# The last splits of two out-projections by token tile, and five products that nothing reads

## The chip, the cores and the metric

One core of a Trainium2 chip runs the whole program. TensorE multiplies and transposes, VectorE and ScalarE compute, GpSimd prepares small tables, and the queue of SyncE starts nearly all transfers from the chip's memory. In the rows they are PE, DVE, ACT, POOL and SP. The metric is the device time of one execution in microseconds (us).

## The reference

Two transformer blocks over 256 tokens of width 1024, all in float32. What matters here of the first block is the way from the heads to the experts:

```python
mixed = jnp.concatenate([rmsnorm(o_m, g_out_mla[i]), rmsnorm(o_s, g_out_sb[i])], axis=-1)
h = h + mixed @ w_o[i]
h = h + moe(rmsnorm(h, g_moe[i]), w_router[i], b_router[i], w_gu[i], b_gu[i], w_dn[i], b_dn[i])
```

`moe` takes 32 router logits of each token, keeps the top four, and applies those experts (1024 to 2048, a clamped SwiGLU, 1024 to 1024), weighted by a softmax of the four logits. Of the second block:

```python
mix = jnp.concatenate([attn, lru], axis=-1) @ w_out[l].astype(h.dtype)
x = x + rms_norm(mix, g_post_mix[l])
h = rms_norm(x, g_pre_ffn[l])
up = causal_dwconv(h @ w_up[l].astype(h.dtype), w_conv_ffn[l], b_conv_ffn[l])
```

## The kernel before

Tokens lie in two tiles of 128 (t = 0, 1), the width in two halves of 512 columns (n = 0, 1), so an out-projection has four results of 128 x 512, one PSUM bank each: `U_o[t][n]` in the first block, `U_mix[t][n]` in the second. The engines run their own instruction lists, each strictly in the order in which it is written, and wait for one another through semaphores.

**Split weights.** A dense product in float32 is made of three fast ones (`mm3`): the weights are a rounded high part and a low part, and so is the other operand. Each load of weights is a "split", numbered 0 to 66 in the order of use. `split(s)` on ACT (L766) writes its high part into one of two halves of the tile W (half s modulo 2), and DVE then writes its low part (L1224). Before `split(s)` writes, it waits for `pair_free[s - 2]`: the last product that reads split s - 2, since both use the same half of W.

**An out-projection** has four splits of two 128-deep slices of the contraction each: 12 to 15 in the first block, 30 to 33 in the second. A split has 24 products (2 slices, 2 token tiles, 2 halves, 3 of `mm3`). `rows_in` runs the first three of them slice by slice over all four results, and the last one result by result (`by_tile`), so that the four results are complete six products apart.

**After the first out-projection** DVE adds each result to `h` (`add_o`, L1491), PE transposes `h` (L2228), ACT and DVE copy the transposes out of PSUM, and PE forms the logits (L2236, 32 columns each). For every token tile DVE finds the top four and writes a mask `mk` (L1526 to L1538, with the semaphore `s_mk`). PE sums the masks into positions (L2245, L2246, L2248), DVE turns them into the selection (L1542, L1564), and with it PE gathers the experts' tokens (L2260) from `uhi` and `ulo`, the high and low parts of the rows that ACT (`rows_hi`, L926) and DVE (`rows_lo`, L1506) write into half 0 and 1 of W. The gathers are followed by `up(x)` (L2293) and `down(x)` (L2333) for each expert x. SP loads the experts' weights into a ring; a place is loaded again when the products that read it have been counted in `s_used`, two slices of 128 to a place.

**After the second out-projection** ACT squares each result with its sum (`square_rows`, L1139) and takes roots (L784, L789), DVE multiplies by the gain (`gained`, L1842), takes the reciprocal and adds to `h` (`add_rows`, L1851). ACT then squares `h` of a token tile (`square_h`, L1147), and its rows are scaled (token tile 0 by ACT, L1156, tile 1 by DVE, L1870), transposed by PE (L2537), and written as high parts by ACT (L1167, 16 times) and low parts by DVE (L1881). From there to the end PE runs the feed-forward part (L2008, L1937). On ACT the call `split(34)`, the first weights of the feed-forward part, stands directly in front of `square_rows` of token tile 0.

## Time and profile before

| | |
|---|---|
| median of 3 runs | 1412.57 us (1411.61 to 1415.88) |
| the profiled execution | 1414.68 us |
| its span | 1412.9 us |
| PE busy | 1285.8 us (91%) |
| DVE busy | 489.1 us (35%) |
| ACT busy | 400.7 us (28%) |
| read from memory | 478.39 MB, 340 GB/s over the span |

The profiled execution is 2.1 us above the median of the runs. Its span leaves out 1.8 us around it. The busy shares are means over stages of different kinds: dense stages with TensorE at work all the time at both ends, and between 360 and about 1070 us a stretch in which the experts' weights flow at 426 to 429 GB/s. The granted clock is a share of 2.4 GHz: 1.00 is 2.4 GHz, 0.50 is 1.2 GHz. PEld is TensorE's loading of the fixed operand.

### The profile page before, as it was taken

Reading aid. Unit: us, or ns where it says so; the run is one execution under the profiler, and the core shown is the slowest. Engines: PE = TensorE matmul, PEld = TensorE weight load, DVE = VectorE, ACT = ScalarE, POOL = GpSimd, SP = SyncE. Lnnn points to the kernel's source line nnn. Section 1 sums busy time; section 2 is a strip of 40 time slices with the busy share of each in tenths; the row PEclk is TensorE's granted clock in tenths of the full one; section 3 lists DMA queues with packets and bytes.
Section 4 is the critical chain, followed back from the end, with each engine's and each line's share of the span. In section 5 each row is a group of like instructions: output and inputs, shape, how many; then the busy total and the mean of one; then the engine's idle time right before and its main releaser. Section 6 shows DMA issues by size and latency. Waiting matters only on the chain.

```text
span 1412.9 us, 16571 instructions
## 1 busy us (share of the span) xinstructions
PE 1285.8 (91%) x6969; PEld 738.8 (52%) x6969; DVE 489.1 (35%) x735; ACT 400.7 (28%) x641; POOL 59.0 (4%) x115
## 2 busy tenths in 40 slices
PE   7989999999999889988888888888888999899998
PEld 7878543333333333333333333333324898799986
DVE  5795412111211112111121111211113777777765
ACT  5674312100111001110010100101003756755554
POOL 4001000000000000000000000000000510000000
PEclk9998899999999999999999999999999999999999
DMA  9437699999999999999999999999999964355520
GB/s 341 166 125 293 228 383 428 430 425 429 427 426 429 427 429 427 427 428 428 426 428 428 427 428 428 427 427 429 427 427 374 264 222 142 126 182 184 189 103 30
DMA packets 78474, 480.79 MB, mean 340 GB/s; under 512 B 5504, under 2 KB 40475, under 8 KB 53568
## 3 DMA queue, kind: packets, MB, share of 16 engines
q1 hardware_dynamic: 75904, 474.76, 82.9%
q0 software_dynamic: 2496, 4.96, 1.6%
q8 instruction: 57, 0.93, 0.3%
q14 instruction: 17, 0.14, 0.0%
HBM read 478.39 MB, written 1.31 MB: 340 GB/s over the span
## 4 chain that ended last, share of the span: by engine, by line
PE 51%; DMA 40%; DVE 4%; ACT 3%; issue 1%; DVEq 0%; SPq 0%; ACTq 0%
DMA arena<-in_w_dn_dram 38%; PE ps L1937 23%; PE ps L2333 11%; PE ps L2293 10%; DMA ring<-in_w_dn_dram 2%; PE ps L2260 1%; PE ps L2349 1%; DVE W L1224 1%; PE ps L1945 1%; PE ps L2450 1%; ACT arena L898 0%; PE ps L2217 0%; ACT arena L947 0%; PE ps L2304 0%; ACT W L766 0%
## 5 line engine op out<-in xcount | busy, mean ns | idle before, releaser
L2293 PE MATMUL ps<-ring,arena 128*64 128x512 f32 x1392 | 315.3, 597 | 11.8 <-DMA ring<-in_w_gu_dram 11.8
L2293 PEld LDWEIGHTS ps<-ring,arena 128*64 128x64 f32 x1392 | 98.7, 137 | 207.9 <-issue 175.4
L1937 PE MATMUL ps<-X,W 128*128 128x256 f32 x1560 | 189.1, 283 | 2.0 <-DVE W L1230 1.7
L1937 PEld LDWEIGHTS ps<-X,W 128*128 128x128 f32 x1560 | 187.8, 192 | 3.1 <-DVE W L1230 2.2
L1573 DVE TENSOR_SCALAR arena<-ps 128x512 f32<-128x512 f32 x32 | 22.1, 692 | 478.3 <-PE ps L2293 478.3
L1937 PE MATMUL ps<-W,X 128*128 128x512 f32 (+2 forms) x780 | 172.7, 381 | 3.8 <-DVE W L1224 1.9
L1224 DVE TENSOR_TENSOR W<-ring,W 128x2048 fp32r<-128x2048 f32 (+2 forms) x64 | 144.9, 2265 | 75.3 <-ACT W L766 75.3
L2333 PE MATMUL ps<-ring,arena 128*64 128x512 f32 x648 | 145.9, 595 | 22.9 <-DMA ring<-in_w_dn_dram 22.9
L1937 PEld LDWEIGHTS ps<-W,X 128*128 128x128 f32 x780 | 142.1, 188 | 31.8 <-DVE W L1224 4.0
L2293 PE MATMUL ps<-arena 128*64 128x512 f32 x656 | 150.5, 601 | 0.0
L960 ACT ACTIVATE arena<-arena 128x512 f32<-128x512 f32 x32 | 20.2, 631 | 459.3 <-DVE arena L1573 459.3
L766 ACT ACTIVATE W<-ring 128x2048 fp32r<-128x2048 f32 (+2 forms) x65 | 122.7, 1888 | 84.1 <-PE ps L1937 83.1
L2333 PEld LDWEIGHTS ps<-ring,arena 128*64 128x64 f32 x648 | 48.4, 137 | 117.6 <-issue 115.8
L2333 PE MATMUL ps<-arena 128*64 128x512 f32 x376 | 85.8, 598 | 24.7 <-DMA arena<-in_w_dn_dram 24.7
L1601 DVE SCALAR_TENSOR_TENSOR X<-ps,arena,X 128x512 fp32r<-128x512 f32 x32 | 24.0, 751 | 221.7 <-ACT X L973 221.7
L973 ACT ACTIVATE X<-ps,arena 128x512 fp32r<-128x512 f32 x32 | 22.0, 689 | 260.4 <-PE ps L2333 260.4
L2293 PEld LDWEIGHTS ps<-arena 128*64 128x64 f32 x656 | 47.5, 138 | 90.9 <-issue 88.7
L2333 PEld LDWEIGHTS ps<-arena 128*64 128x64 f32 x376 | 25.1, 136 | 84.9 <-DMA arena<-in_w_dn_dram 43.2
L2260 PEld LDWEIGHTS ps<-X,W 128*128 128x128 f32 x256 | 33.9, 198 | 25.5 <-issue 24.9
L714 POOL CAST W<-arena 128x128 fp32r<-128x128 f32 x32 | 9.4, 296 | 870.0 <-PE ps L2293 852.1
L2349 PE MATMUL ps<-X,W 64*128 64x512 f32 x256 | 39.3, 425 | 6.5 <-DVE X L1601 6.5
L2304 PE MATMUL ps<-ident,arena 128*128 128x128 f32 x128 | 21.4, 291 | 25.6 <-ACT arena L947 25.6
(348 smaller groups left out, 996.6 us busy)
## 6 DMA issues: line engine op xcount, KB each, us to landing
ring<-in_w_gu_dram SPq DMA_DIRECT2D x87, 2048.0 KB, 22.4
ring<-in_w_dn_dram SPq DMA_DIRECT2D x40, 2048.0 KB, 24.9
arena<-in_w_gu_dram SPq DMA_DIRECT2D x39, 2048.0 KB, 20.6
arena<-in_w_dn_dram SPq DMA_DIRECT2D x23, 2048.0 KB, 25.6
ring<-in_w_up_dram SPq DMA_DIRECT2D x22, 1024.0 KB, 5.1
ring<-in_w_in_dram SPq DMA_DIRECT2D x15, 1024.0 KB, 12.9
ring<-in_w_down_dram SPq DMA_DIRECT2D x11, 1024.0 KB, 4.9
ring<-in_w_o_dram SPq DMA_DIRECT2D x4, 1024.0 KB, 5.0
```

The lines of the kernel that those rows point to most:

```text
L766: e.activation(halved(s)[0], loads[n][0], ACT.Copy).then_inc(s_hi, 1)
L960: e.activation(sig, glu, ACT.Sigmoid, scale=1.702).then_inc(s_sig, 1)
L973: e.activation(yhi[x % 2], ps[:, DB, :], ACT.Copy, scale=gs[:, x:x + 1]).then_inc(s_yhi, 1)
L1224: e.tensor_tensor(lo, loads[SPL[s]][0], hi.bitcast(F32), ALU.subtract).then_inc(s_lo, 1)
L1573: e.tensor_scalar(glu, whole(gb), 7.0, None, ALU.min).then_inc(s_glu, 1)
L1601: e.scalar_tensor_tensor(out=ylo[x % 2], in0=ps[:, DB, :], scalar=gs[:, x:x + 1], in1=yhi[x % 2].bitcast(F32), op0=ALU.mult, op1=ALU.subtr ...
L1937: y = e.matmul(o, l, r, start=start and i == 0, stop=stop and i == 2)
L2260: y = e.matmul(ps[:, x[0], a * 256:(a + 1) * 256], part[:, t, k * P:(k + 1) * P], Sr[j % 2][:, t], start=part is uhi and t == 0, stop=part ...
L2293: y = e.matmul(ps[c * 64:c * 64 + 64, use[0], :], xs[:, k, c0:c0 + CAP], w[:, half * D + c * 512:half * D + (c + 1) * 512], start=False, s ...
L2304: y = e.transpose(ps[:, TB, j * P:(j + 1) * P], actv[:, j * P:(j + 1) * P], ident[:, :])
L2333: y = e.matmul(ps[c * 64:c * 64 + 64, DB, :], a, w[:, c * 512:(c + 1) * 512], start=kk == 0, stop=kk == KD - 1)
L2349: y = e.matmul(ps[:, b, :], GTr[x // 2 % 2][q, x % 2, t * P:(t + 1) * P], part[x % 2][q, :], start=x == 0 and part is yhi, stop=x == NE - ...
```

## The change

Three things are changed.

1. **First out-projection.** Splits 14 and 15 are run by token tile: on three results (0,0), (0,1), (1,0) split 14 and then split 15, then the eight transposes of token tile 0, and only then splits 14 and 15 on (1,1). The other transposes stand around the first half of the logits. DVE and ACT take their steps in a matching order, and `rows_hi` waits until split 14 has been read for the last time.
2. **Five products that nothing reads** (`kept_busy`): 128x128 by 128x512, from `uhi`, into a bank that a later gather overwrites. Two stand between the mask products of token tile 0 and that of tile 1, three behind the latter.
3. **Second out-projection.** Splits 32 and 33 are run in the same way, without anything between. The squares of `h` of token tile 0 stand between those of the results (1,0) and (1,1), with semaphores of their own.

```diff
@@ -1144,18 +1147,19 @@
             def square_h(t):
                 for n in range(2):
                     e.wait_ge(*BK.emptied(U_mix[t][n]))
-                e.activation(u[:, t, :], h[:, t, :], ACT.Square, accum_out=ss[:, t:t + 1]).then_inc(squares.sem, 1)
...
             square_rows("mix", 0, U_mix)
             root_rows("mix", 0)
-            square_rows("mix", 1, U_mix)
+            square_rows("mix", 1, U_mix, (0,))
+            square_h(0)
+            root(1, 2, D, ffn_squares["ffn", 0], ss[:, 0:1], done=ffn_roots.sem)
+            square_rows("mix", 1, U_mix, (1,))
             root_rows("mix", 1)
-            square_h(0)
-            root(1, 2, D, squares["ffn", 0], ss[:, 0:1])
             e.wait_ge(s_r0, 1)
             e.activation(u[:, 0, :], h[:, 0, :], ACT.Copy, scale=rs[:, 2:3]).then_inc(s_u0, 1)
             square_h(1)
-            root(1, 3, D, squares["ffn", 1], ss[:, 1:2])
+            root(1, 3, D, ffn_squares["ffn", 1], ss[:, 1:2], done=ffn_roots.sem)
 
 
...
             add_o(0, 0)
             add_o(0, 1)
+            scaled(0)
             add_o(1, 0)
+            turned_out(0)
             add_o(1, 1)
 
 
-            scaled(0)
-            turned_out(0)
+            rows_lo(0, slice(0, 512), 1)
             turned_out(1)
-            rows_lo(0, slice(0, 512), 1)
+            scaled(1)
             e.wait_ge(s_brt, 16)
             e.wait_ge(*pool["i32", 0])
             for t in range(2):
-                if t:
...
-            gained_rows("mix", 1, U_mix, gmix)
+            gained("mix", 1, 0, U_mix, gmix)
+            e.wait_ge(*ffn_roots["ffn", 0])
+            e.reciprocal(rs[:, 2:3], rs[:, 2:3]).then_inc(s_r0, 1)
+            gained("mix", 1, 1, U_mix, gmix)
             over_root("mix", 1, 1, 1)
-            add_rows(1, 0, U_mix)
-            e.wait_ge(*roots["ffn", 0])
-            e.reciprocal(rs[:, 2:3], rs[:, 2:3]).then_inc(s_r0, 1)
-            add_rows(1, 1, U_mix)
+            for n in range(2):
+                add_rows(1, n, U_mix)
             hi, lo = halved(34)
             e.wait_ge(s_hi, 35)
             e.tensor_tensor(lo[:, 0:4], loads[SPL[34]][0][:, 0:4], hi[:, 0:4].bitcast(F32), ALU.subtract)
...
+            def rows_part(s, ks, t, n, uses, x_ready, last):
+
+                hi, lo = halved(s)
+                e.wait_ge(*lo_done(s))
+                use, c = uses[t][n], slice(n * 512, (n + 1) * 512)
+                for i, k in enumerate(ks):
+                    e.wait_ge(*x_ready(k))
+                    y = mm3(whole(use), [z[:, k, t * P:(t + 1) * P] for z in xin], (hi[:, i, c], lo[:, i, c]), False,
+                            last and k == ks[-1], True)
+                if last:
+                    y.then_inc(full[use[0]], 1)
                 return y
...
             rows_in(13, (6, 7), 0, U_o, xin, 4, 3, 512, 1024, sT_ready).then_inc(s_pair, 1)
-            rows_in(14, (0, 1), 0, U_o, xin, 4, 3, 512, 1024, mT_ready).then_inc(s_pair, 1)
-            rows_in(15, (2, 3), 0, U_o, xin, 4, 3, 512, 1024, mT_ready, by_tile=True)
+            for t, n in ((0, 0), (0, 1), (1, 0)):
+                rows_part(14, (0, 1), t, n, U_o, mT_ready, False)
+            for t, n in ((0, 0), (0, 1), (1, 0)):
+                rows_part(15, (2, 3), t, n, U_o, mT_ready, True)
...
+            turned_rows(0, 0)
+            turned_rows(0, 1)
+            rows_part(14, (0, 1), 1, 1, U_o, mT_ready, False).then_inc(s_pair, 1)
+            rows_part(15, (2, 3), 1, 1, U_o, mT_ready, True)
...
+            turned_rows(1, 0)
...
             for t in range(2):
...
+                        if k and t == 0:
+                            turned_rows(1, 1)
...
+            def kept_busy(n):
+
+                for _ in range(n):
+                    e.matmul(whole(U_gath[0, 3]), uhi[:, 0, 0:P], uhi[:, 0, 0:512], start=True, stop=True)
+
             claim(U_pos)
+            claim(U_gath[0, 3])
+            e.wait_ge(s_uhi, 1)
             e.wait_ge(s_mk, 1)
...
             e.matmul(ps[:, b, 0:NE], tri, mk[:, 0, :], start=True, stop=True)
             e.matmul(ps[:, b, NE:2 * NE], bc(onec, [P, P]), mk[:, 0, :], start=True, stop=False)
+            kept_busy(2)
             e.wait_ge(s_mk, 2)
             e.matmul(ps[:, b, NE:2 * NE], tri, mk[:, 1, :], start=False, stop=True).then_inc(full[b], 1)
+            kept_busy(3)
...
             rows_in(31, (6, 7), 0, U_mix, xin, 4, 3, 512, 1024, mix_ready).then_inc(s_pair, 1)
-            rows_in(32, (0, 1), 0, U_mix, xin, 4, 3, 512, 1024, mix_ready).then_inc(s_pair, 1)
-            rows_in(33, (2, 3), 0, U_mix, xin, 4, 3, 512, 1024, mix_ready, by_tile=True)
+            for t, n in ((0, 0), (0, 1), (1, 0)):
+                rows_part(32, (0, 1), t, n, U_mix, mix_ready, False)
+            for t, n in ((0, 0), (0, 1), (1, 0)):
+                rows_part(33, (2, 3), t, n, U_mix, mix_ready, True)
+            rows_part(32, (0, 1), 1, 1, U_mix, mix_ready, False).then_inc(s_pair, 1)
+            rows_part(33, (2, 3), 1, 1, U_mix, mix_ready, True)
...
```

On PE, from the first out-projection to the first gather. L2228 and L2240 are the transposes, L2236 and L2265 the logits, L2217 and L2252 the bias of expert 0, L2245 to L2248 and L2282 to L2286 the mask products. Before:

```order
90 L1937 MATMUL ps<-W,X 128x512 x72
91 L2228 MATMUL ps<-ident,h 128x128 x16
92 L2236 MATMUL ps<-wr,arena 128x32 x16
93 L2217 MATMUL ps<-X,W 128x512 x2
94 L2245 MATMUL ps<-arena 128x32
95 L2246 MATMUL ps<-arena,sm 128x32
96 L2248 MATMUL ps<-arena 128x32
97 L2260 MATMUL ps<-X,W 128x256 x16
```

The change:

```order
91 L2240 MATMUL ps<-ident,h 128x128 x8
92 L1943 MATMUL ps<-W,X 128x512 x12
93 L2240 MATMUL ps<-ident,h 128x128 x4
94 L2265 MATMUL ps<-wr,arena 128x32 x4
95 L2240 MATMUL ps<-ident,h 128x128 x4
96 L2265 MATMUL ps<-wr,arena 128x32 x12
97 L2252 MATMUL ps<-X,W 128x512 x2
98 L2282 MATMUL ps<-arena 128x32
99 L2283 MATMUL ps<-arena,sm 128x32
100 L2274 MATMUL ps<-W 128x512 x2
101 L2286 MATMUL ps<-arena 128x32
102 L2274 MATMUL ps<-W 128x512 x3
```

Of the 72 products of splits 13 to 15 the last 12 now stand behind eight transposes, and the logits of token tile 0 are begun before the last four transposes. The rows of L2274 are the five new products.

On ACT, from split 34 to the squares of `h` of token tile 1; `s_w_pair` is what the splits wait for. L766 and L768 are the split, L1139 and L1142 the squares of the four results, L1147 and L1150 those of `h`. Before:

```order
397 L766 ACTIVATE W<-ring 128x2048 [waits s_land4,s_w_pair]
398 L1139 ACTIVATE arena,sm<-ps 128x512 [waits s_full6]
399 L789 ACTIVATE sm<-sm 128x1 [waits s_squares]
400 L1139 ACTIVATE arena,sm<-ps 128x512 [waits s_full7]
401 L784 ACTIVATE sm<-sm 128x1 [waits s_squares,s_half_means]
402 L1139 ACTIVATE arena,sm<-ps 128x512 [waits s_full0]
403 L789 ACTIVATE sm<-sm 128x1 [waits s_squares]
404 L1139 ACTIVATE arena,sm<-ps 128x512 [waits s_full1]
405 L784 ACTIVATE sm<-sm 128x1 [waits s_squares,s_half_means]
406 L1147 ACTIVATE arena,sm<-h 128x1024 [waits s_out7,s_out6]
407 L784 ACTIVATE sm<-sm 128x1 [waits s_squares]
408 L1156 ACTIVATE arena<-h,sm 128x1024 [waits s_ffn_root0]
```

The change:

```order
397 L768 ACTIVATE W<-ring 128x2048 [waits s_land4,s_w_pair]
398 L1142 ACTIVATE arena,sm<-ps 128x512 [waits s_full6]
399 L791 ACTIVATE sm<-sm 128x1 [waits s_squares]
400 L1142 ACTIVATE arena,sm<-ps 128x512 [waits s_full7]
401 L786 ACTIVATE sm<-sm 128x1 [waits s_squares,s_half_means]
402 L1142 ACTIVATE arena,sm<-ps 128x512 [waits s_full0]
403 L791 ACTIVATE sm<-sm 128x1 [waits s_squares]
404 L1150 ACTIVATE arena,sm<-h 128x1024 [waits s_out7,s_out6]
405 L786 ACTIVATE sm<-sm 128x1 [waits s_ffn_squares]
406 L1142 ACTIVATE arena,sm<-ps 128x512 [waits s_full1]
407 L786 ACTIVATE sm<-sm 128x1 [waits s_squares,s_half_means]
408 L1160 ACTIVATE arena<-h,sm 128x1024 [waits s_ffn_root0]
```

The split and its wait stand where they stood, ahead of the first square; the square of `h` of token tile 0 has moved ahead of that of the result (1,1).

On PE, the second out-projection from split 32 on (`s_w_lo` is the low part of a split, one wait for each call). Before:

```order
1433 L1937 MATMUL ps<-W,X 128x512 [waits s_out2,s_w_lo]
1434 L1937 MATMUL ps<-W,X 128x512 x11
1435 L1937 MATMUL ps<-W,X 128x512 [waits s_out2]
1436 L1937 MATMUL ps<-W,X 128x512 x11
1437 L1937 MATMUL ps<-W,X 128x512 [waits s_out3,s_w_lo]
1438 L1937 MATMUL ps<-W,X 128x512 x2
1439 L1937 MATMUL ps<-W,X 128x512 [waits s_out3]
1440 L1937 MATMUL ps<-W,X 128x512 x2
```

The change, split 32 on the three results and then split 33 on the first; (1,0) and (1,1) follow in the same way:

```order
1455 L1943 MATMUL ps<-W,X 128x512 [waits s_out2,s_w_lo]
1456 L1943 MATMUL ps<-W,X 128x512 x2
1457 L1943 MATMUL ps<-W,X 128x512 [waits s_out2]
1458 L1943 MATMUL ps<-W,X 128x512 x2
1459 L1943 MATMUL ps<-W,X 128x512 [waits s_out2,s_w_lo]
1460 L1943 MATMUL ps<-W,X 128x512 x2
1461 L1943 MATMUL ps<-W,X 128x512 [waits s_out2]
1462 L1943 MATMUL ps<-W,X 128x512 x2
1463 L1943 MATMUL ps<-W,X 128x512 [waits s_out2,s_w_lo]
1464 L1943 MATMUL ps<-W,X 128x512 x2
1465 L1943 MATMUL ps<-W,X 128x512 [waits s_out2]
1466 L1943 MATMUL ps<-W,X 128x512 x2
```

Split 32 was read through by its 24th product, ahead of all products of split 33; now its last six products stand behind 18 of split 33.

## Rows read from the trace of the kernel before

**Rows 1.** the page, part 4: the chain that ended last, by line
```profile
DMA arena<-in_w_dn_dram 38%; PE ps L1937 23%; PE ps L2333 11%; PE ps L2293 10%; DMA ring<-in_w_dn_dram 2%; PE ps L2260 1%; PE ps L2349 1%; DVE W L1224 1%; PE ps L1945 1%; PE ps L2450 1%; ACT arena L898 0%; PE ps L2217 0%; ACT arena L947 0%; PE ps L2304 0%; ACT W L766 0%
```

**Rows 2.** the chain in order of time: start us, us, what
```profile
360.72 24.88 DMA ring<-in_w_dn_dram
...
1225.44 120.96 PE ps L1937 x1008
```

**Rows 3.** windows: us, busy of PE, PEld, DVE, ACT, POOL, granted clock, DMA share, GB/s
```profile
144.50:146.20 1.70, 1.30 (x12) 1.22 (x11) 1.51 (x7) 1.70 (x4) 0.00 (x0) 0.96 0.00 0
146.50:151.80 5.30, 3.84 (x15) 3.40 (x16) 3.72 (x13) 3.80 (x4) 0.00 (x0) 0.50 0.52 185
151.80:156.00 4.20, 4.20 (x18) 3.75 (x20) 2.49 (x5) 1.25 (x4) 0.00 (x0) 0.50 0.06 21
...
165.00:200.00 35.00, 34.01 (x173) 13.40 (x172) 9.77 (x18) 6.35 (x11) 1.29 (x3) 1.00 0.98 381
200.00:360.00 160.00, 155.17 (x739) 60.32 (x740) 25.59 (x42) 21.76 (x39) 1.78 (x6) 0.98 1.00 424
```

**Rows 4.** timeline of PE, first out-projection to first gather: start us, us, instruction
```profile
124.57 16.78 PE L1937 MATMUL ps<-W,X 128*128 128x512 f32 x72
...
142.93 1.87 PE L2236 MATMUL ps<-wr,arena 128*128 128x32 f32 x16
145.20 2.80 PE L2236 MATMUL ps<-wr,arena 128*128 128x32 f32 x16 [0.40 <-ACT arena L933]
147.81 1.20 PE L2217 MATMUL ps<-X,W 128*128 128x512 f32 x2
...
149.87 0.64 PE L2248 MATMUL ps<-arena 128*128 128x32 f32 x2 [0.17 <-DVE arena L1538]
151.81 3.75 PE L2260 MATMUL ps<-X,W 128*128 128x256 f32 x16 [1.30 <-DVE X L1564]
...
159.46 1.22 PE L2260 MATMUL ps<-X,W 128*128 128x256 f32 x8
```

**Rows 5.** timeline of DVE, first out-projection to selection
```profile
132.27 2.29 DVE L1224 TENSOR_TENSOR W<-ring,W 128x2048 fp32r<-128x2048 f32 x1 [2.16 <-ACT W L766]
...
148.10 0.25 DVE L1526 SCALAR_TENSOR_TENSOR arena<-ps,sm 128x32 f32<-128x32 f32 x1 [1.38 <-PE ps L2236]
...
149.45 0.37 DVE L1538 TENSOR_REDUCE arena<-arena 128x32 f32<-128x128 f32 x1
...
151.01 0.69 DVE L1564 TENSOR_TENSOR X<-sm 128x512 fp32r<-128x512 f32 x1
```

**Rows 6.** timeline of the queue of SP: the first load of the down-projection
```profile
159.57 5.06 SPq L641 DMA_DIRECT2D ring<-in_w_dn_dram  x2
```

**Rows 7.** timeline of ACT, second out-projection
```profile
1204.86 1.92 ACT L766 ACTIVATE W<-ring 128x2048 fp32r<-128x2048 f32 x1 [2.00 <-PE ps L1937]
1206.69 0.57 ACT L1139 ACTIVATE arena<-ps 128x512 f32<-128x512 f32 x1
...
1211.29 1.04 ACT L1147 ACTIVATE arena<-h 128x1024 f32<-128x1024 f32 x1
...
1215.40 4.46 ACT L1167 ACTIVATE X<-ps,cols 128x128 fp32r<-128x128 f32 x16
```

**Rows 8.** timeline of PE, second out-projection
```profile
1193.66 16.61 PE L1937 MATMUL ps<-W,X 128*128 128x512 f32 x72
1214.18 1.76 PE L2537 MATMUL ps<-ident,arena 128*128 128x128 f32 x8 [3.91 <-ACT arena L1156]
1216.53 1.72 PE L2537 MATMUL ps<-ident,arena 128*128 128x128 f32 x8 [0.59 <-DVE arena L1870]
...
1219.91 5.53 PE L2008 MATMUL ps<-X,W 128*128 128x256 f32 x44 [0.23 <-ACT X L1167]
```

**Rows 9.** timeline of DVE, second out-projection
```profile
1201.38 2.29 DVE L1224 TENSOR_TENSOR W<-ring,W 128x2048 fp32r<-128x2048 f32 x1 [2.87 <-ACT W L766]
1207.48 1.52 DVE L1842 TENSOR_TENSOR arena<-ps,arena 128x512 f32<-128x512 f32 x2 [3.81 <-ACT arena L1139]
...
1209.10 1.42 DVE L1851 SCALAR_TENSOR_TENSOR h<-arena,sm,h 128x512 f32<-128x512 f32 x2
```

**Rows 10.** windows of the second out-projection, columns as in rows 3
```profile
1214.50:1217.50 3.00, 2.41 (x13) 2.01 (x11) 2.16 (x4) 2.97 (x11) 0.00 (x0) 0.50 0.00 0
```

43 lines of the change are left out of this document (24 added, 19 removed).

## The prediction

> **What bounds the kernel now.** I read the summary of the chain first, then the chain in time, then the two places of the change engine by engine. Of the chain 38% is the transfer of the experts' down-projection weights [rows 1]. The chain in time shows where: the first such wait stands at 360.7 us, and from 1225.4 us on it is TensorE's products without a break [rows 2]. Between 360 and about 1070 us TensorE waits for the weights of each expert. Does a gain ahead of that stretch come through? The queue issues the first down-projection load at 159.57 us, when TensorE has read the first two slices of expert 0 [rows 6]. From 165 us the transfers are busy for 0.98 and from 200 us for 1.00 of the time [rows 3]. The stream is full from about there on, has a fixed amount to bring and starts when TensorE frees the first place. So I take what is gained at the first gathers one to one to the end. In the second place nothing is hidden: TensorE waits 3.91 us for the rows of token tile 0 and 0.59 us for those of tile 1 [rows 8], and then works to the end [rows 2].
>
> **The second out-projection.** This is the larger term, and a loss. TensorE's 72 products of splits 31 to 33 run from 1193.7 to 1210.3 us [rows 8], 0.23 us each. Split 32 ends 24 products before that end, at 1204.8. ACT's split 34, which overwrites the half of W that split 32 is read from, starts right then, at 1204.86 [rows 7]; the first square starts at 1206.69, when the split lets ACT go.
>
> The change moves the last six products of split 32 behind 18 of split 33. Split 33 is also wanted sooner, 18 instead of 24 products into the last 48: at 1203.45, while its low part is written until 1203.67 [rows 9]. That adds 0.25 us. Split 32 is then read through at 1203.7 + 24 x 0.2275 = 1209.2. The split 34 still stands ahead of all squares on ACT and still waits for that. It starts 4.4 us later, at 1209.25, and the first square at 1211.1. Queued behind it are all four squares, and behind those DVE's gains and additions. The results (0,0), (0,1) and (1,0) are complete 1.1 us sooner than before, but nobody can take them up.
>
> Up to the addition to token tile 0 both programs do the same steps, which end at 1209.10 + 1.42 = 1210.5 before [rows 9], so at 1214.9 now. From there to the first of ACT's 16 copies at 1215.40 [rows 7] it was 4.9 us. Now the square of `h` (1.04 us [rows 7], about 1.2 to its root and 0.2 more to the next instruction) comes ahead of the square of (1,1), which takes 0.8 us with its sum, and its root 0.3. Then follow a reciprocal (0.45 with its waits), the two additions (1.42 [rows 9]) and the last square and root (1.37 up to the copy, as before). That is 5.75 us, so the first copy moves to 1220.7. TensorE's transposes of tile 1 move by the same 5.3 us, from 1216.5 to 1221.8, and ACT's 4.46 us of copies [rows 7] gate the feed-forward part as they do now: **+5.3 us**. DVE's low part of split 34 and ACT's split 35 keep their places relative to it and hide as before.
>
> The clock adds to this. It was at 0.50 from 1214.5 to 1217.5, after 3.9 us without a product, and TensorE was busy for 2.41 of those 3.0 us when it came back [rows 8, 10]. Now TensorE stands still for 8 us (1210.5 to 1218.5), and its transposes come with more air between them. Either the clock is back when the dense products start at 1225.2, which costs nothing, or they begin at half rate. The 44 products took 5.53 us at full clock [rows 8]; half rate through about 3 us of them costs 1.5. I take 0.7. Behind the rows stands a rule, Part 4 (PE-mode transpose) of "TensorE: Matmul & The Clock Gate" in the Trainium skill: transposes do not bring the full clock back. The trace disagrees, since here the clock returned with only transposes behind it. By the page the loss would be the full 1.5 us and the sum 0.8 us higher. Against the change speaks also the same page's line on queues in Part 1, that ACT takes its instructions strictly in order. The trace agrees: the square of (0,0) waited out the split.
>
> **The first out-projection.** The same order costs less there, since no split stands behind 14 and 15. The low part of split 15 ends at 134.56 [rows 5] and is wanted at 134.45: 0.15 us. The eight transposes put in take 0.95 us, so the last result is complete at 142.4 instead of 141.3 [rows 4]. Its addition, the last transposes and the logits follow. In exchange tile 0's root, reciprocal and copies are off the way. Following each engine in its new order I get tile 0's logits at 145.2 and tile 1's at 147.0 at full clock, 147.5 at half; DVE read the latter at 148.10 [rows 5]. The mask of tile 1 comes 1.72 us behind them: at 148.8 or 149.3 instead of 149.82 [rows 5]. From there to the first gather it was 2.0 us (151.81 [rows 4]), for DVE's `rows_lo`, positions and selection.
>
> The clock decides what this is worth. In the trace it fell at about 146.2, when TensorE had had only transposes and 32-column products since 141.3 with hardly a gap (1.30 of 1.70 us busy), and it was at 0.50 until 156.0 [rows 3]. Between 151.8 and 156.0 dense gathers ran at half rate: 16 took 3.75 us, 8 at full clock 1.22 [rows 4]. The half clock costs about 2.2 us there. The five new products are the first 512-column work in the gap. None stands before 147 us, so they come after the fall, not ahead of it. One lasts 0.23 us at full clock; at half clock, by the gather (16 of 256 columns in 3.75 us [rows 4]), 0.47. At half clock the two in the middle are not hidden: bias 1.2 [rows 4], first mask products 0.9 and the two 0.9 end at 150.3, a full microsecond behind the mask. The last mask product (0.64 [rows 4]) then ends at 150.9, the selection at 151.9, and the three others let the gather go at 152.3, 0.5 us later than now. But the array has then been busy with wide work since about 149.4, so I expect the clock back 1 to 3 us sooner, saving 1.1 to 2.2 of the 2.2 us. At full clock all through the gather starts at 150.8 and saves both, 1.0 + 1.9. Bounds: -2.9 and +0.5. I take **-1.2**, since the rows show the clock falling before the first new product.
>
> **Sum.** +5.3 + 0.7 - 1.2 = +4.8 us: 1419.5 against the profiled execution's 1414.68. That one lies 2.1 us above the median of 1412.57, against which I predict **1417.4 us**. About 0.3% (4.2 us) is what a measurement of this kernel can tell from no change; the bounds are 1408.3 and 1416.8.
>
> **Rivals.**
> *B, the clock holds.* The place is the first: the new order spreads wide products (142.4 us instead of 141.3 is the last one), and with the five the clock doesn't fall or falls only for a moment. Price: -2.9 there, +5.3 in the second place, +2.4 in all: 1415.0, not slower by what can be told. It decides when TensorE's clock stays at 2.4 GHz up to the first gather. For it speaks that both falls in the trace came 4 to 5 us after the last wide product; against it that tile 0's narrow work still lasts until 147 us.
> *C, the fillers hold the selection up.* At half clock they cost 0.5 us and the clock returns no sooner; in the second place the feed-forward part starts at half rate (+1.5). +0.5 + 5.3 + 1.5 = +7.3: 1419.9.
> *D, ACT is not held.* If split 34 found its half of W free in time, squares would start when the results are complete; only (1,1), 0.25 us late, would count, and the square of `h` taken early would save about 0.5 us. With -1.2 to -2.9 of the first place: 1410.0. The order of the instructions speaks against it: the wait is there, and its last product has moved by 18 products.
> *E, the first gain is lost in the stream.* If the transfers did not start sooner, A becomes +6.0: 1418.6. The idle transfers before 159.57 us (0.06 of the time from 151.8 to 156 [rows 3]) speak against it.
>
> **How the numbers follow.** A (the forecast) 0.48, B 0.20, C 0.16, E 0.08, D 0.08. A spreads from 1415.8 to 1419, so about 0.6 of it is slower by over 0.3%; so are C, E and little of B: 0.29 + 0.16 + 0.07 + 0.02 = 0.54. Faster than 1408.3 is left only to D at its far end with the first place at its best: 0.03. The rest, 0.43, is within 0.3%. The range from 1413.8 to 1421.0 holds A, B, C and E with a microsecond for the runs, whose own span before was 4.3 us, and leaves out D.
>
> **What would show it.** In the changed profile: ACT's split 34 starts about 4.4 us later against the end of split 31; the first square starts after the last product of split 33; TensorE idles some 8 us there instead of 3.9. At the first place, the granted clock between the last result and the second gather, and the first down-projection load's issue against the start of the span (1 to 3 us sooner). If split 34 starts where it did, or if the squares start one by one as the results come, the main term is wrong. If the load at 159.6 moves and the transfer stream ends where it did, the one to one is wrong.

## The result, and the profile after

Over 20 runs each the changed kernel took 1416.27 us in the median (1413.16 to 1420.26), the kernel before 1412.61 us (1409.53 to 1416.02). The ratio is 1.0025, with a 95% interval of 1.0017 to 1.0033: the change makes the kernel 3.5 us slower (2.4 to 4.7 by the interval; the medians differ by 3.7). The forecast was 1417.4 us, 1413.8 to 1421.0. The profiled execution of the changed kernel has a span of 1416.8 us, that of before 1412.9.

The loss is in the second out-projection, as the experiments confirm. TensorE in the changed kernel, columns as in [rows 8]:

```profile
1190.81 9.81 PE L1943 MATMUL ps<-W,X 128*128 128x512 f32 x42
1200.88 7.10 PE L1943 MATMUL ps<-W,X 128*128 128x512 f32 x30 [0.26 <-DVE W L1228]
1215.90 1.97 PE L2580 MATMUL ps<-ident,arena 128*128 128x128 f32 x8 [7.93 <-ACT arena L1160]
1219.28 1.97 PE L2580 MATMUL ps<-ident,arena 128*128 128x128 f32 x8 [1.41 <-DVE arena L1876]
1221.72 7.63 PE L2027 MATMUL ps<-X,W 128*128 128x256 f32 x48 [0.47 <-ACT X L1171]
```

The 72 products are there in two pieces, with 0.26 us of waiting for the low part of split 33 between them. Behind them TensorE stands still for 7.93 us where it stood still for 3.91 [rows 8]. The releaser in both is ACT's write to the normalised `h` (`arena`, L1160). So the place to look at is ACT, columns as in [rows 7]:

```profile
1206.65 1.92 ACT L768 ACTIVATE W<-ring 128x2048 fp32r<-128x2048 f32 x1 [6.64 <-PE ps L1943]
1208.47 0.57 ACT L1142 ACTIVATE arena<-ps 128x512 f32<-128x512 f32 x1
...
1212.38 1.06 ACT L1150 ACTIVATE arena<-h 128x1024 f32<-128x1024 f32 x1 [1.04 <-DVE h L1854]
...
1213.76 0.58 ACT L1142 ACTIVATE arena<-ps 128x512 f32<-128x512 f32 x1
...
1218.15 4.46 ACT L1171 ACTIVATE X<-ps,cols 128x128 fp32r<-128x128 f32 x16
```

ACT's split 34 (L768) waited 6.64 us for TensorE and started 15.84 us after the first product of split 31; before it was 11.20 us ([rows 7, 8]), 4.6 us less. The square of (0,0) (L1142) starts when the split lets ACT go, at 1208.47, though its result was complete some 5.9 us earlier. (Where nothing held the squares, in an experiment below, the first of them started 1.70 us after the second piece of the products: 1201.71 less 1200.01. Here that would be 1202.6.) DVE shows the same hold from the other side (start, us, instruction):

```profile
1209.27 1.49 DVE L1845 TENSOR_TENSOR arena<-ps,arena 128x512 f32<-128x512 f32 x2 [8.45 <-ACT arena L1142]
...
1210.87 1.41 DVE L1854 SCALAR_TENSOR_TENSOR h<-arena,sm,h 128x512 f32<-128x512 f32 x2
```

Its gains (L1845) were idle for 8.45 us ahead of them, released by ACT; in [rows 9] it was 3.81. From the first square to the first of the 16 copies (L1171) it is now 9.68 us, before 8.71 [rows 7].

In the first out-projection things moved the other way, by about a microsecond. TensorE, from the first product of split 13 on, to be held against [rows 4]:

```profile
123.56 14.45 PE L1943 MATMUL ps<-W,X 128*128 128x512 f32 x60
...
145.78 0.71 PE L2252 MATMUL ps<-X,W 128*128 128x512 f32 x2
...
146.76 1.20 PE L2274 MATMUL ps<-W 128*128 128x512 f32 x2
...
148.21 1.63 PE L2274 MATMUL ps<-W 128*128 128x512 f32 x3
149.72 3.76 PE L2299 MATMUL ps<-X,W 128*128 128x256 f32 x16
```

The gather starts 26.16 us after the first product of split 13 (149.72 less 123.56), before 27.24 (151.81 less 124.57). L2274 are the five products that nothing reads. The queue of SP, as in [rows 6]:

```profile
157.13 5.06 SPq L643 DMA_DIRECT2D ring<-in_w_dn_dram  x2
```

That is 33.57 us after the first product of split 13, before 35.00. The granted clock (windows, columns as in [rows 3]):

```profile
143.00:146.40 3.40, 3.40 (x32) 3.21 (x29) 3.14 (x12) 3.37 (x6) 0.00 (x0) 1.00 0.02 5
147.00:153.00 6.00, 6.00 (x22) 4.81 (x23) 5.14 (x10) 2.70 (x5) 0.00 (x0) 0.50 0.46 171
153.50:157.00 3.50, 3.50 (x16) 0.97 (x16) 0.00 (x0) 0.84 (x2) 0.00 (x0) 1.00 0.00 0
1212.00:1225.00 13.00, 7.22 (x31) 6.41 (x32) 11.05 (x28) 11.40 (x28) 0.00 (x0) 0.50 0.25 81
1225.50:1229.00 3.50, 3.50 (x32) 3.50 (x31) 1.23 (x1) 0.97 (x3) 0.00 (x0) 1.00 0.29 88
```

It fell at 146.7 us, before at 146.1, and was back at 153.5, before at 156.3. The two unread products at 146.76 are both at half rate: 1.20 us, where the two of the same size at 145.78 took 0.71. In the second place the clock was at 0.50 from 1211.6 to 1225.3, through the transposes and the first part of the dense products; before it was so from 1214.4 to 1217.9. The first 48 of these took 7.47 us to the start of the next (1221.72 to 1229.19); before it was 6.31 (1218.97 to 1225.28).

### The profile page after: what moved, and what is told of

It reads as the page before. It is cut to its first block, busy times and chain, and to the rows that moved or that the text cites. A ratio compares the mean times of both kernels' runs of the same rounds, so it can differ in the third digit from the quotient of the medians.

```text
span 1416.8 us, 16598 instructions
## 1 busy us (share of the span) xinstructions
PE 1286.2 (91%) x6974; PEld 736.2 (52%) x6974; DVE 489.0 (35%) x735; ACT 400.2 (28%) x641; POOL 59.0 (4%) x115
## 4 chain that ended last, share of the span: by engine, by line
PE 52%; DMA 39%; DVE 5%; ACT 3%; issue 1%; DVEq 0%; SPq 0%; ACTq 0%
DMA arena<-in_w_dn_dram 36%; PE ps L1943 22%; PE ps L2332 11%; PE ps L2372 11%; DMA ring<-in_w_dn_dram 2%; DVE W L1228 1%; PE ps L2299 1%; ACT W L768 1%; PE ps L2388 1%; PE ps L2489 1%; PE ps L2027 1%; PE ps L2252 1%; PE ps L2183 0%; ACT arena L950 0%; PE ps L2343 0%
## 5 line engine op out<-in xcount | busy, mean ns | idle before, releaser
L2372 PE MATMUL ps<-ring,arena 128*64 128x512 f32 x648 | 145.9, 595 | 23.4 <-DMA ring<-in_w_dn_dram 23.4
L1943 PEld LDWEIGHTS ps<-W,X 128*128 128x128 f32 x780 | 141.5, 188 | 34.0 <-DVE W L1228 6.1
L768 ACT ACTIVATE W<-ring 128x2048 fp32r<-128x2048 f32 (+2 forms) x65 | 122.7, 1887 | 88.2 <-PE ps L1943 87.8
```

The costliest lines, as they stand in the source:

```text
L768: e.activation(halved(s)[0], loads[n][0], ACT.Copy).then_inc(s_hi, 1)
L1943: y = e.matmul(o, l, r, start=start and i == 0, stop=stop and i == 2)
L2372: y = e.matmul(ps[c * 64:c * 64 + 64, DB, :], a, w[:, c * 512:(c + 1) * 512], start=kk == 0, stop=kk == KD - 1)
```

## The experiments

Times are medians. Ratios are to the kernel before, run beside them on the same chip: 1412.61 us for the change itself, then 1414.27 us for the next four rows, 1413.92 for the four behind them and 1413.58 for the last three. A ratio is not the quotient of the two medians, and they can differ by 0.1%: by the medians the second place alone stands at 1.0029 and the first alone at 0.9985. The last three columns are each from one profile. The stretch called the first stage runs from the first product of split 13 to the issue of the first down-projection load, and the copy offset from the first product of split 31 to ACT's first of 16 copies. I use these stretches since split 13 itself starts anywhere from 121.3 to 124.6 us in different profiled executions, with the same instructions ahead of it. "The five" are the unread products of the change.

| kernel | ratio (95%) | first stage, us | copy offset, us | first 48 dense products, us |
|---|---|---|---|---|
| before | 1 | 35.00 | 21.74 | 6.31 |
| the change | 1.0025 (1.0017 to 1.0033) | 33.57 | 27.34 | 7.47 |
| second place alone | 1.0037 (1.0024 to 1.0050) | 34.06 | 27.33 | 7.70 |
| the same, split 34 later | 1.0005 (0.9996 to 1.0014) | 33.56 | 23.42 | 7.82 |
| first place alone | 0.9992 (0.9977 to 1.0007) | 33.38 | 21.74 | 7.19 |
| the change, split 34 on GpSimd | 0.9994 (0.9984 to 1.0004) | 33.54 | 21.91 | 8.47 |
| first place, none of the five | 0.9997 (0.9987 to 1.0007) | 33.77 | 21.74 | 7.81 |
| steps of ACT and DVE alone | 1.0009 (0.9998 to 1.0019) | 33.94 | 22.73 | 7.75 |
| second place alone, 32 unread products | 1.0033 (1.0022 to 1.0044) | 34.04 | 27.33 | 8.38 |
| first place, 14 unread in the second | 0.9985 (0.9972 to 0.9997) | 33.69 | 21.75 | 7.31 |
| first place, 48 unread for three | 1.0070 (1.0055 to 1.0084) | 42.46 | 21.74 | 7.86 |
| first place, 14, 5 and 4 unread in the second | 0.9982 (0.9973 to 0.9991) | 33.59 | 21.74 | 6.31 |
| the change, split 34 later | 0.9988 (0.9976 to 1.0000) | 32.01 | 23.40 | 7.54 |

### Which place pays: the second alone, and the first alone

The second place alone is the changed kernel with the first out-projection, the vector steps behind it and the logits as before and without the five products (two waits that the change added stay, for split 14 ahead of the rows and for the rows ahead of the mask products):

```diff
-            for t, n in ((0, 0), (0, 1), (1, 0)):
-                rows_part(14, (0, 1), t, n, U_o, mT_ready, False)
...
+            rows_in(14, (0, 1), 0, U_o, xin, 4, 3, 512, 1024, mT_ready).then_inc(s_pair, 1)
+            rows_in(15, (2, 3), 0, U_o, xin, 4, 3, 512, 1024, mT_ready, by_tile=True)
...
-            kept_busy(2)
...
-            kept_busy(3)
```

> The second out-projection as changed, the first one as before, no unread products. Theory (ACT is held by split 34): +5.3 us from the chain of steps, plus 0.7 to 2 us for a feed-forward part that begins at half clock: +6 to +7.5 us against the kernel before, ratio 1.0042 to 1.0053. Split 34 starts about 9.9 us after the first product of split 32 instead of 5.5. Rival (the loss sits in the first place, where the fillers delay the selection): under +2 us here.

Measured: 1418.37 us, ratio 1.0037, so +5.2 us (3.4 to 7.1; by the medians +4.1), a little less than expected. ACT in this kernel, columns as above:

```profile
1204.57 1.92 ACT L768 ACTIVATE W<-ring 128x2048 fp32r<-128x2048 f32 x1 [6.63 <-PE ps L1944]
...
1216.06 4.46 ACT L1171 ACTIVATE X<-ps,cols 128x128 fp32r<-128x128 f32 x16
```

The hold is the same as in the whole change (6.63 us of waiting for TensorE ahead of the split), and the copy offset is 27.33 us against 27.34.

The first place alone keeps the new order of the first out-projection and the five products, and puts splits 32 and 33 and the steps of ACT and DVE back:

```diff
-            for t, n in ((0, 0), (0, 1), (1, 0)):
-                rows_part(32, (0, 1), t, n, U_mix, mix_ready, False)
...
+            rows_in(32, (0, 1), 0, U_mix, xin, 4, 3, 512, 1024, mix_ready).then_inc(s_pair, 1)
+            rows_in(33, (2, 3), 0, U_mix, xin, 4, 3, 512, 1024, mix_ready, by_tile=True)
```

> The first out-projection and the five unread products as changed, the second out-projection as before. Theory: -1.2 to -2.9 us, and the first down-projection load is issued that much sooner after split 13 begins. The trace of the change gave -1.4 for that stretch. If the experts' transfers do not pass the gain on: 0. If the fillers hold the selection up: +0.5.

Measured: 1412.17 us, ratio 0.9992, so -1.1 us (-3.3 to +1.0; by the medians -2.1). The two add up to +4.1 us (+2.0 by the medians), against +3.5 (2.4 to 4.7) for the whole change. So the loss, 4 to 5 us, is in the second place. In the first there is at most a small gain, which this measurement alone can't tell from nothing.

### What in the second place pays: the split, taken out of the way

> As second_only, but ACT's split 34 stands behind the square of the result (1,0) instead of ahead of all squares; nothing else moves. If holding ACT is the cause, the squares of (0,0) to (1,0) run while split 32 is still read, and most of the loss goes: 4 us less than second_only, +1 to +2.5 us against before. If the products' order itself or the 0.25 us wait for the low part of split 33 were the cause, it stays at second_only's +6.

```diff
             prime(ACT.Sqrt)
-            split(34)
...
             square_rows("mix", 0, U_mix)
             root_rows("mix", 0)
             square_rows("mix", 1, U_mix, (0,))
+            split(34)
             square_h(0)
```

Measured: 1414.64 us, ratio 1.0005 (0.9996 to 1.0014). One moved line takes 4.5 of the 5.2 us away by the ratios, 3.7 by the medians; what is left is +0.7 us (-0.6 to +2.0), less than the +1 to +2.5 expected. ACT shows how, columns as before:

```profile
1201.71 0.60 ACT L1141 ACTIVATE arena<-ps 128x512 f32<-128x512 f32 x1 [2.56 <-PE ps L1944]
...
1203.07 0.60 ACT L1141 ACTIVATE arena<-ps 128x512 f32<-128x512 f32 x1 [0.35 <-PE ps L1944]
...
1204.43 0.60 ACT L1141 ACTIVATE arena<-ps 128x512 f32<-128x512 f32 x1 [0.28 <-PE ps L1944]
...
1205.79 1.92 ACT L768 ACTIVATE W<-ring 128x2048 fp32r<-128x2048 f32 x1 [0.34 <-PE ps L1944]
...
1213.37 4.46 ACT L1171 ACTIVATE X<-ps,cols 128x128 fp32r<-128x128 f32 x16
```

The squares now start one by one 1.36 us apart, as the results come, each with a short wait for TensorE. The split stands behind three of them and starts at 1205.79, when its half of W is read through; (1,1) waits for it. The first copy moves from 27.33 to 23.42 us, so 3.9 of the 5.6 us by which it had moved come back. The products stand in the same order as in the run before; it is the instruction at the head of ACT's order that makes the loss.

Of the other 1.7 us of the copy offset 1.5 are the split, which is still ahead of the last square: with the split on GpSimd, below, the offset is 21.91 us. The steps of ACT and DVE in their new order were taken alone: splits 32 and 33 as before, only the order of the vector engines' steps as changed.

```diff
-            square_rows("mix", 1, U_mix)
+            square_rows("mix", 1, U_mix, (0,))
+            square_h(0)
+            root(1, 2, D, ffn_squares["ffn", 0], ss[:, 0:1], done=ffn_roots.sem)
+            square_rows("mix", 1, U_mix, (1,))
             root_rows("mix", 1)
-            square_h(0)
-            root(1, 2, D, squares["ffn", 0], ss[:, 0:1])
```

> The kernel before with one part of the second place: ACT and DVE take the square of h of token tile 0 ahead of the square of the result (1,1), while the products of splits 32 and 33 and the place of split 34 stay as before. Theory: this reordering alone is the 0.9 us of my +5.3: the stretch from split 31's first product to ACT's first copy goes from 21.7 us to 22.4 to 22.9, and the time rises by 0.7 to 1.2 us. Rival (the steps overlap and the reordering is free): no change.

Measured: 1413.79 us, ratio 1.0009 (0.9998 to 1.0019), which can't be told from no change; the copy offset is 22.73 us against 21.74: +0.99.

```profile
1206.60 1.06 ACT L1150 ACTIVATE arena<-h 128x1024 f32<-128x1024 f32 x1 [0.65 <-DVE h L1855]
...
1207.98 0.58 ACT L1142 ACTIVATE arena<-ps 128x512 f32<-128x512 f32 x1
...
1212.37 4.46 ACT L1171 ACTIVATE X<-ps,cols 128x128 fp32r<-128x128 f32 x16
```

The square of `h` (1206.60) goes ahead of the square of (1,1) (1207.98). The latter, with its root, reciprocal and the two additions, lies on the way to the last row, and the square of `h` does not.

### Is it the work of the split, or its place in ACT's order?

In the whole change the high part of split 34 was given to GpSimd, which has nothing to do there:

```diff
+            w34 = loads[SPL[34]]
+            e.wait_ge(*pair_free[32])
+            e.wait_ge(s_land[w34[2]], 16 * w34[4])
+            e.tensor_copy(halved(34)[0], w34[0]).then_inc(s_hi, 1)
...
             prime(ACT.Sqrt)
-            split(34)
...
+            e.wait_ge(s_hi, 35)
             split(35)
```

> The whole change, but the high part of split 34 is written by GpSimd, which has nothing to do there, so ACT takes the squares as the results come. Theory: the second place gives -0.5 us instead of +6.6, the first -1.4: 1410.5 us, ratio 0.9985, if GpSimd writes the 128x2048 in under 4 us. It would be near +1 if GpSimd needs over 6 us (its 128x1024 products of two operands took 2.4 us in the profile), since the low part waits for it.

Measured: 1413.17 us, ratio 0.9994 (0.9984 to 1.0004), where 0.9985 was expected. GpSimd's timeline and ACT's:

```profile
1207.23 1.93 POOL L755 CAST W<-ring 128x2048 fp32r<-128x2048 f32 x1 [37.99 <-PE ps L1947]
```

```profile
1203.12 0.60 ACT L1145 ACTIVATE arena<-ps 128x512 f32<-128x512 f32 x1 [2.56 <-PE ps L1947]
...
1207.51 1.06 ACT L1153 ACTIVATE arena<-h 128x1024 f32<-128x1024 f32 x1 [0.65 <-DVE h L1858]
...
1208.89 0.58 ACT L1145 ACTIVATE arena<-ps 128x512 f32<-128x512 f32 x1
...
1213.28 4.46 ACT L1174 ACTIVATE X<-ps,cols 128x128 fp32r<-128x128 f32 x16
```

The copy takes 1.93 us there, as long as on ACT, and no square waits for it. The copy offset is 21.91 us: the copies start only 0.2 us later than before, and the 0.5 us that I had expected the second place to gain is not there. The offsets from the first product of split 31 (1191.37 here) show why. The first square starts at 11.75 us, where it was 13.03 [rows 7, 8]: the results do come one by one, 1.3 us sooner. But the last result, (1,1), cannot come sooner by an order of the same products, and comes later by TensorE's wait in the middle of them: the 72 products end 17.15 us after the first began (1201.43 + 7.09 less 1191.37), before 16.61. Its square starts at 17.52 us (1208.89), held by the square of `h` (1207.51) too; before it started at 16.64 (1210.30 in the trace of before). From there to the copies it is 4.39 us here and 5.10 before. What the early squares give is given away at the last one. Behind the copies this profile's clock did worse as well: the first 48 dense products took 8.47 us, and the next one started 33.95 us after the first product of split 31, against 31.62 to 33.17 in the four profiles with the place as before and nothing filled.

### What the clock does in the second place

> As second_only, with 32 unread 128x512 products (7.3 us at full clock) in the 7.9 us in which TensorE waits for the rows of token tile 0. It measures the clock's share of the loss. Theory: the clock stays at 1.00 through the transposes, the first 48 products of the feed-forward part take 5.5 us instead of 7.9, the transposes of tile 1 end 0.5 us sooner, and the time falls by 2 to 3 us against second_only. If the clock cost nothing: no change, or a loss where the 32 run into the transposes.

The edit, in the second place alone: 32 products of 512 columns that nothing reads, ahead of the transposes of token tile 0.

```diff
+            claim(U_fT[0][0])
+            for _ in range(32):
+                e.matmul(whole(U_fT[0][0]), xin[0][:, 0, 0:P], X[:, 0, 0:2, :].rearrange("p k t -> p (k t)"), start=True, stop=True)
             for t in range(2):
                 if t == 0:
                     e.wait_ge(s_u0, 1)
```

Measured: 1417.76 us, ratio 1.0033 (1.0022 to 1.0044), against 1.0037 without them: of the 2 to 3 us expected nothing is seen. TensorE and the windows:

```profile
1207.20 7.42 PE L2567 MATMUL ps<-X 128*128 128x512 f32 x32
1215.30 1.09 PE L2577 MATMUL ps<-ident,arena 128*128 128x128 f32 x8 [0.69 <-ACT arena L1160]
1218.68 1.09 PE L2577 MATMUL ps<-ident,arena 128*128 128x128 f32 x8 [2.28 <-DVE arena L1877]
1220.88 8.54 PE L2028 MATMUL ps<-X,W 128*128 128x256 f32 x48 [1.11 <-ACT X L1171]
```

```profile
1215.30:1219.50 4.20, 1.92 (x16) 1.68 (x16) 3.70 (x6) 3.31 (x11) 0.00 (x0) 1.00 0.00 0
1220.00:1226.00 6.00, 5.12 (x23) 5.11 (x24) 6.00 (x17) 5.06 (x10) 0.00 (x0) 0.50 0.54 175
```

The gap was filled (7.42 us of products in place of a wait), and the clock stayed at 1.00 through them and through the transposes, eight of which took 1.09 us here and 1.97 at half clock. But ahead of the second eight transposes and of the dense products TensorE still waited, 2.28 and 1.11 us. The clock fell at 1219.7, at the end of these transposes, and the dense products began at half rate: 8.38 us for the first 48, more than without the filling (7.70). Filling this gap alone did not keep the clock for the dense products.

> As first_only (second place as in the kernel before), with 14 unread products (3.2 us) in the 3.9 us gap of the second place. Theory: the clock stays up there and the feed-forward part starts at full rate, which first_only's profile did not (7.35 us for its first 48 products instead of 5.5): 0.5 to 2 us faster than first_only, 1 to 3 us faster than before (ratio 0.998 to 0.9993).

```diff
+            for _ in range(14):
+                e.matmul(whole(U_fT[0][0]), xin[0][:, 0, 0:P], X[:, 0, 0:2, :].rearrange("p k t -> p (k t)"), start=True, stop=True)
```

This is the same with 14 products, in the first place alone, where the gap is 3.9 us. Measured: 1411.88 us, ratio 0.9985 (0.9972 to 0.9997), against 0.9992 without. The first 48 dense products took 7.31 us against 7.19. The clock stayed at 1.00 through the first eight transposes and fell at 1215.4, behind the second eight. By the two intervals this is no difference either, and the 5.5 us expected for the dense products are missed.

> As first_only, with unread products in all three waits of the second place: 14 ahead of the transposes of token tile 0, 5 between the two sets of transposes, 4 ahead of the feed-forward part. In the profile of second_warm the clock held through the 7.4 us of unread products and fell during the transposes and the waits between them. Theory: with all waits filled it stays at 1.00, the first 48 products take 5.5 us instead of 7.2 to 7.8, and the time is 2.5 to 4 us under the kernel before (ratio 0.997 to 0.998), 1 to 2 us under first_warm. Rival (transposes alone bring the clock down): no better than first_warm.

Here all three gaps are filled, with products from the high part of split 34 that go to the bank of `U_cv[2]`: 14 ahead of the transposes of tile 0, 5 ahead of those of tile 1, 4 ahead of the dense products.

```diff
+            def spare(n):
+                for _ in range(n):
+                    e.matmul(whole(U_cv[2]), W[:, 0, 0, 0:P], W[:, 0, 0, 0:512], start=True, stop=True)
...
+            spare(14)
...
+                    spare(5)
...
+            spare(4)
```

```profile
1206.44 3.33 PE L2567 MATMUL ps<-W 128*128 128x512 f32 x14
...
1211.37 1.41 PE L2567 MATMUL ps<-W 128*128 128x512 f32 x5
...
1213.72 1.17 PE L2567 MATMUL ps<-W 128*128 128x512 f32 x4
...
1216.01 5.53 PE L2025 MATMUL ps<-X,W 128*128 128x256 f32 x44 [0.23 <-ACT X L1170]
```

```profile
1206.00:1222.00 16.00, 14.76 (x96) 12.53 (x95) 13.96 (x31) 13.49 (x32) 0.00 (x0) 1.00 0.22 71
```

The clock was at 1.00 from 1206 to 1222 us, and 44 dense products took 5.53 us. Measured: 1411.12 us, ratio 0.9982 (0.9973 to 0.9991). That is the fastest kernel of this study, 2.5 us under the one before (1.3 to 3.8), and 1.4 us under the first place alone by the ratios; the intervals of these two overlap, so what is measured as a gain over the kernel before is the first place and the filled gaps together. Nor can it be told from the kernel with the 14 alone (0.9985), where 1 to 2 us were expected. One profile shows the clock kept with all three gaps filled; that this shortens the execution is not shown.

The table above shows one more thing. The kernel before, and those with the second place as before, run the same instructions there. The first 48 dense products took 6.31 us in the profile of the kernel before, and 7.19, 7.81 and 7.86 in the three others without filling. In these the clock fell between 1.1 us ahead of the first transposes and 0.9 us behind their start, in that of before 0.3 us behind it; but it came back only 3.0 to 4.5 us behind the first dense product, where in the profile of before it was back 1.1 us ahead of it. So the profile of before, on which I had based the clock term, had drawn a short fall.

### What the five products do

> As first_only without the five unread products. In the profiles so far the three kernels with the new first place took 33.4 to 33.6 us from the first product of split 13 to the first down-projection load, and their clock came back 3.6 us after the first gather began. Theory (the dense gather brings the clock back, the five come too late to matter): the same stretch at 33.4 to 33.8 us and the same time as first_only within 0.5 us. Rival (the five hold or restore the clock): 1 to 2 us longer, up to 35.5.

```diff
-            kept_busy(2)
...
-            kept_busy(3)
```

Measured, in the first place alone: 1413.13 us, ratio 0.9997 (0.9987 to 1.0007), against 0.9992 (0.9977 to 1.0007) with them. Windows with the five, then without:

```profile
140.00:149.40 9.40, 8.46 (x60) 7.08 (x58) 8.04 (x23) 7.92 (x10) 0.53 (x2) 1.00 0.54 209
150.00:153.00 3.00, 3.00 (x15) 2.90 (x14) 2.08 (x5) 0.84 (x2) 0.00 (x0) 0.50 0.03 8
153.50:156.00 2.50, 2.50 (x14) 0.86 (x12) 0.00 (x0) 0.57 (x2) 0.00 (x0) 1.00 0.00 0
```

```profile
140.00:147.00 7.00, 7.00 (x55) 6.41 (x53) 5.78 (x16) 5.77 (x9) 0.53 (x2) 1.00 0.44 185
148.00:153.80 5.80, 4.29 (x18) 3.99 (x18) 4.61 (x9) 2.17 (x4) 0.00 (x0) 0.50 0.39 161
154.50:157.00 2.50, 2.50 (x14) 0.84 (x12) 0.00 (x0) 0.28 (x1) 0.00 (x0) 1.00 0.00 0
```

In this pair the clock fell at 149.7 us with the five and at 147.6 without. But four other profiles with the five had the fall earlier, at 146.6 to 147.5, ahead of the five or during the first two of them: 23.1 to 23.4 us after the first product of split 13, and 23.6 without the five. So the pair doesn't show that the five hold the clock. It came back at 153.1 in the one and 154.5 in the other, 3.5 and 4.3 us after the gather's start (149.55 and 150.15), and 3.8 to 4.2 us after it in the four others. The 16 gather products took 3.64 and 3.75 us, and the gather began 26.1 us after the first product of split 13 with and without the five. By the first stage the five are worth 0.4 us in this pair (33.38 against 33.77), which no run here can tell from nothing. That they hold the clock in some executions is not excluded: the one profile below in which it never fell has them.

### Does a shift in the first place come through to the end?

> As first_only, with 48 unread products behind the last mask product instead of three: the first gather is held back. It asks whether time at the first gathers comes one to one to the end. 48 products last 10.9 us at full clock; less the wait they fill (1.7 us after the mask) and the 1.2 to 2 us that the gather gains at full clock, the first down-projection load should be issued 8 to 11 us later against split 13 than in first_only. One to one: the time rises by the same, 8 to 11 us. If the stream of weights absorbs it: 0 to 4 us.

```diff
-            kept_busy(3)
+            kept_busy(48)
```

```profile
148.09 12.21 PE L2272 MATMUL ps<-W 128*128 128x512 f32 x48
160.13 2.07 PE L2297 MATMUL ps<-X,W 128*128 128x256 f32 x16
```

```profile
165.93 5.05 SPq L643 DMA_DIRECT2D ring<-in_w_dn_dram  x2
```

Measured: 1422.15 us, ratio 1.0070 (1.0055 to 1.0084). The load is issued 9.1 us later than in the first place alone (156.82), split 31 starts 9.3 us later (1199.10 against 1189.78), and the median is 10.0 us longer (by the two ratios 11.0, 8.1 to 13.9). So the stream of weights takes up nothing of this shift that can be seen: it comes through one to one. (A gain of a microsecond was too small to test in the same way.) The 48 also brought the clock back ahead of the gather, at 150.3 us, and the 16 gather products took 2.07 us at full rate.

### The whole change with the split moved

> The whole change with one line moved: split 34 on ACT behind the square of (1,0). Theory: the change's +3.7 us minus the 3.9 us that the same move took from second_only in the profile: between -1.5 and +0.5 us against before, ratio 0.999 to 1.0003. If the loss were somewhere else: still 1.0025.

```diff
-            split(34)
...
             square_rows("mix", 1, U_mix, (0,))
+            split(34)
             square_h(0)
```

Measured: 1411.83 us, ratio 0.9988 (0.9976 to 1.0000): 5.2 us less than the change by the ratios, more than the 3.9 expected, and 1.7 less than the kernel before, just at the edge of what can be told. Its profile has one more thing, in the first place:

```profile
140.00:156.00 16.00, 14.89 (x95) 10.74 (x94) 11.46 (x29) 9.96 (x15) 0.53 (x2) 1.00 0.39 152
```

In this execution the clock did not fall there at all, and the first stage took 32.01 us, 1.5 less than the 33.55 us that the five others with the same code there took in the mean. The edit touches nothing ahead of 1190 us, so whether the clock falls there varies between executions with the same code up to that place.

## Why the prediction was right, point by point

**The hold of split 34: right, in mechanism and size.** Predicted +4.4 us on its start; it was 4.6. The wait for the low part of split 33 (predicted 0.25) cost 0.56: the 72 products now end 17.17 us after the first began (1200.88 + 7.10 less 1190.81), before 16.61. I had set the end of the low part against the end that the profile gives the product ahead, and not against the start of the next one, which comes sooner. The moved line and GpSimd's copy both take the hold away, and the time goes with it.

**The steps of ACT and DVE: right.** Predicted 0.9 us (5.75 for 4.9); measured 0.97 in the change from the first square to the first copy, and 0.99 alone. Together the first copy moved by 5.6 us where I had 5.3.

**The clock in the second place: right for the trace it was made against, too large as a term.** I took +0.7. Between the two profiles it was +1.2 (7.47 against 6.31). But four kernels with the place as before and unfilled took 6.31, 7.19, 7.81 and 7.86, 7.3 in the mean, and the two with the hold 7.47 and 7.70: +0.3. The step that failed is "It was at 0.50 from 1214.5 to 1217.5", read as the kernel's habit where it was one execution's. Of the Trainium skill, "TensorE: Matmul & The Clock Gate", Part 4, I had written that the trace disagrees with it on transposes. That needs a second half. In the profile of before the full clock came back at 1217.9 us, with only transposes since its fall. In three others with the same code there it did not come back until dense products had run for 3.0 to 4.5 us, and in the one with 32 unread products it was lost at the end of the transposes, as the page would have it. No run here isolates transposes from the gaps between them.

**The first place: sign right, size a little too large.** I took -1.2 against the profile of before, between -2.9 and +0.5. The two profiles differ by 1.43 us in the first stage, but that of before was a long one: with the old order there the stage took 34.12 us in the mean of five profiles, with the new and the five products 33.30 in six, so -0.8, and the first place alone was measured at -1.1 (-3.3 to +1.0). Without the odd profile on either side, that of before and the one in which the clock never fell, it is 33.90 against 33.55, only -0.35: more of the gain in the profiles is the clock's scatter than the new order. The step that failed is "I expect the clock back 1 to 3 us sooner": counted from the first product of split 13 it came back at 29.9 us where it was 31.7 in the trace of before, 1.8 us sooner; but without the five it came back at 30.4, so 1.3 of this is not theirs. And the gather starts only 0.3 us sooner by the steps (26.1 us after split 13 began, 26.4 in all profiles with the old order but that of before, which had 27.24; there the 16 products of the second logits took 2.80 us [rows 4], partly at half clock, and 1.94 in the others).

**One to one: right,** shown by the delay for a shift of 9 us.

**The rivals.** B, the clock holds in the first place, was not what the change's own profile shows, but one profile of six with that code did it, at 1.5 us less in the first stage. C, the fillers hold the selection up, fell: the selection (DVE's L1567, 148.92 and 0.69 us) ended at 149.6 us, the gather started at 149.7 behind the last of the three, and without the five it started as late, 26.1 us after the first product of split 13. D, ACT is not held, fell with the 6.64 us in front of the split. E, the gain lost in the stream, fell with the delay.

**The number.** The sum was +4.8 us and the measured difference +3.5 (2.4 to 4.7). The parts that the runs give are +5.2 and -1.1, together +4.1. Of the 1.3 us that the sum has too many, 0.4 is the clock term; the rest is within the interval. It is not accounted for, though: put together from the profiles, the copies' 5.6 us, the clock's 0.3 and the first stage's -0.8 make +5.1, above the interval. What makes the execution 0.4 us or more shorter than that is open. At 0.25% the difference lies inside my bound of 0.3% for what counts as the same (0.43), and the interval reaches past it (to 0.33%), the side on which I had put 0.54. That the sum came out this near is in part luck: the clock term was 0.4 too high and the -1.2 of the first place, read against one long profile, up to 0.8 too low, and these two work against each other.

## What to carry to other kernels

When products are put in another order so that results come one by one, look at who else waits for the operands that now are read until later: an overwrite of a weight buffer that stands at the head of an in-order engine holds all that is queued behind it, and the new order then makes it worse than the old. Move the overwrite behind the first consumers or to an idle engine, and ask what the last result gains; here it came no sooner, and so the end didn't either. A gap filled with unread products bought nothing here that could be told while unfilled ones stood behind it, and with all of them filled only the clock of one profile shows an effect.

## What the runs showed of the hardware that I had not expected

- The granted clock's fall and return differ between executions of the same code. The same 48 products behind the second place as before took from 6.31 to 7.86 us, and the first stage of the changed order was 1.5 us shorter in the one profile in which the clock never fell. By these two spreads I estimate the uncertainty of a term read from one profile's clock at about a microsecond per place.
- The clock can fall while TensorE is busy. In the changed kernel the profile has it busy for all of the 3.40 us from 143.0 to 146.4, and the clock fell at 146.7; what it had done since 141.5 were transposes, 32-column products and two wide ones (145.78). The clock came back 3.8 us after the start of the dense gather, and in the other profiles that fell there and had no more than the five unread products ahead 3.0 to 4.5 us after it.
- GpSimd's copy of 128x2048 values to fp32r took 1.93 us in its one profile, ACT's 1.92.
- A wait in the middle of a dense run of 128x512 products cost more than the profile counts as idle: 0.26 us of idle time, and 17.17 us for 72 products in place of 16.61. The profile's ends of products are modelled, and idle time is counted from them.
